# One-hot columns made by ScalarE alone, GpSimd left with gathers, and coefficient lines written at the head of their step

## The reference, cut to what matters

```python
def peer_ffn(h, w_q, sub_keys, u_tab, v_tab):
    q = einsum('bsd,dk->bsk', h, w_q)                  # 8 heads, two halves of 128
    scores = einsum('bshcd,hcnd->bshcn', q, sub_keys)  # 128 keys for each half
    s1, i1 = top_k(scores[..., 0, :], 16)
    s2, i2 = top_k(scores[..., 1, :], 16)
    top_s, pos = top_k(s1[..., :, None] + s2[..., None, :], 16)
    ids = i1 * 128 + i2                                # at pos
    gates = softmax(top_s)
    act = gelu(einsum('td,tkd->tk', hx, u_tab[ids])) * gates
    return einsum('tk,tkd->td', act, v_tab[ids])
```

## Time and profile before

| | us |
|---|---|
| median of 3 runs | 3553.94 |
| lowest and highest | 3546.19, 3554.21 |
| the profiled execution | 3556.24 |
| its span in the trace | 3554.20 |
| first step of `build_experts` to the end of step 17 | 993 to 1562 |
| steps 6 to 14 (groups and quads) | 1120 to 1478 |
| steps 15 to 17 (groups alone) | 1478 to 1562 |

### The profile page before, as it was taken

The page is one execution under the profiler, slowest core; times in us unless marked ns, Lnnn a source line. Parts: engine busy times, 40 slices in busy tenths (PEclk is TensorE's granted clock), DMA queues, the critical chain, the costliest instruction groups (busy, mean ns, idle before and its releaser), DMA issues.

```text
span 3554.2 us, 32041 instructions
## 1 busy us (share of the span) xinstructions
PE 2922.2 (82%) x10195; PEld 1434.4 (40%) x10195; DVE 1954.6 (55%) x4610; ACT 558.1 (16%) x1043; POOL 1588.2 (45%) x1444
## 2 busy tenths in 40 slices
PE   8999999785245766666758999989999899998997
PEld 3455455443122333443323444434444344443333
DVE  2334433787579777867874656645556444443103
ACT  1321133221002444640000000000000000000000
POOL 0010011334434555454456565555666566664441
PEclk9999969877577888777879999999999999999998
DMA  2100121444687888679899999999999999998993
GB/s 102 46 24 24 37 74 51 146 146 144 225 299 252 307 305 318 232 268 372 311 344 405 397 404 401 402 349 391 389 404 374 356 394 401 402 406 343 336 349 117
DMA packets 307573, 981.52 MB, mean 276 GB/s; under 512 B 29904, under 2 KB 57680, under 8 KB 306640
## 3 DMA queue, kind: packets, MB, share of 16 engines
q0 software_dynamic: 184320, 671.17, 50.2%
q1 hardware_dynamic: 120464, 307.85, 22.9%
q10 hardware_dynamic: 2624, 0.46, 0.1%
HBM read 941.63 MB, written 37.75 MB: 276 GB/s over the span
## 4 chain that ended last, share of the span: by engine, by line
PE 25%; DMA 16%; DVE 11%; POOL 11%; issue 7%; ACT 1%; DVEq 1%; ACTq 0%; SPq 0%; another core or an unknown queue 0%; POOLq 0%
DMA v_ring<-in_peer_v_dram,ids_t 11%; PE part L1703 8%; PE hid L1684 7%; PE acc L1736 6%; POOL v_ring L1630 5%; POOL u_ring L1621 4%; DVE u_ring L1976 4%; DMA u_ring<-in_peer_u_dram,ids_u 3%; PE turn_ps L1676 3%; POOL dense_sums L1652 1%; PE part L1712 1%; DMA wq_pair<-in_peer_wq_dram 1%; DVE scratch_later L1215 1%; DVE scratch_later L1213 1%; DVE idx_later L1162 1%
## 5 line engine op out<-in xcount | busy, mean ns | idle before, releaser
L1976 DVE CUSTOM_DVE_ANT_0 u_ring<-u_ring,x_rows_in 128x1024 f32<-128x1024 f32 x560 | 678.1, 1227 | 511.2 <-DMA u_ring<-in_peer_u_dram,ids_u 477.9
L1630 POOL DMA_INDIRECT v_ring<-in_peer_v_dram,ids_t x640 | 678.8, 1061 | 577.1 <-PE acc L1736 415.5
L1621 POOL DMA_INDIRECT u_ring<-in_peer_u_dram,ids_u x560 | 620.4, 1108 | 461.2 <-DVE dots L1976 325.7
L1703 PE MATMUL part<-room 128*128 128x512 f32 x1536 | 694.6, 603 | 83.9 <-DVE room L1956 76.5
L1684 PE MATMUL hid<-x1t_dense,room 128*128 128x384 f32 x2048 | 703.5, 497 | 10.8 <-DMA room<-in_peer_ut_dram 9.0
L1684 PEld LDWEIGHTS hid<-x1t_dense,room 128*128 128x128 f32 x2048 | 386.9, 193 | 349.2 <-issue 107.1
L1736 PE MATMUL acc<-v_ring,line 128*32 128x512 f32 x2560 | 350.2, 669 | 184.7 <-DMA v_ring<-in_peer_v_dram,ids_t 132.2
L1703 PEld LDWEIGHTS part<-room 128*128 128x128 f32 x1536 | 292.8, 193 | 445.7 <-issue 343.1
L1799 ACT ACTIVATE room<-hid 128x384 f32<-128x384 f32 x128 | 62.7, 490 | 1555.3 <-PE hid L1684 1368.4
L1966 DVE TENSOR_TENSOR dense_sums<-dense_sums,part 128x512 f32<-128x512 f32 x186 | 125.6, 685 | 297.3 <-PE part L1703 258.9
L1736 PEld LDWEIGHTS acc<-v_ring,line 128*32 128x32 f32 x2560 | 75.7, 117 | 398.7 <-issue 338.3
(11 more groups left out here) (312 smaller groups left out, 2734.8 us busy)
## 6 DMA issues: line engine op xcount, KB each, us to landing
wq_pair<-in_peer_wq_dram SPq DMA_DIRECT2D x32, 2048.0 KB
room<-in_peer_ut_dram SPq DMA_DIRECT2D x128, 512.0 KB
room<-in_peer_v_dram SPq DMA_DIRECT2D x128, 512.0 KB
gate_grid<-room SPq DMA_DIRECT2D x6, 4096.0 KB, 15.1
room<-gate_grid SPq DMA_DIRECT2D x32, 768.0 KB
w_ring<-in_w_in_dram SPq DMA_DIRECT2D x5, 2048.0 KB, 8.0
v_ring<-in_peer_v_dram,ids_t POOLq DMA_INDIRECT x640
u_ring<-in_peer_u_dram,ids_u POOLq DMA_INDIRECT x560
```

The source lines that it names most:

```text
L1621: pool.indirect_dma_start(u_ring[:, n % U_RING, :], None, peer_u, bass.IndirectOffsetOnAxis(ap=ids_u[:, q, k:k + 1], axis=0))\
L1630: pool.indirect_dma_start(v_ring[:, n % V_RING, :], None, peer_v, bass.IndirectOffsetOnAxis(ap=ids_t[:, q % 2, token:token + 1], axis=0))\
L1703: last = mm.matmul(part[k % 3][:], weights[:, n % 2, i, d * P:(d + 1) * P], vd[:, slot, half * 512:(half + 1) * 512], start=(i == 0), stop ...
L1976: vec.tensor_tensor_reduce(u_ring[:, n % U_RING, :], u_ring[:, n % U_RING, :], x1[:, q % 2, :], 1.0, 0.0, ALU.mult, ALU.add, dots[:, q % 2 ...
```

## The change

- GpSimd's subtraction (L1652) and its semaphore are gone. GpSimd's program in `build_experts` holds gathers and nothing else after its constants.
- `parts_t` now holds i1, the gate and minus i2, in this order. The third is copied out of PSUM with scale -1 by an instruction of its own, so there are two copies for a dense tile where there was one.
- `mark_i2` makes |0..127 - i2| by ScalarE alone: four instructions of 128x128, one for each token, with the token's column of minus i2 as bias, and then the relu over 128x512 as before. It waits for the group three before to have been built instead of for GpSimd.
- A line other than a tile's first is written at the head of the step that holds its first quad, ahead of everything else that ScalarE does in that step. A tile's first line stays where it was, since its coefficients come only in the same quarter.
- ScalarE waits at its start for the seventh constant, the row 0..127.

```diff
-                    for k in share(token_groups(s), i, PARTS):
-                        d, at = k // QUADS, (k % QUADS) * 4
-                        pool.wait_ge(parts_t_ready, d + 1)
-                        if k >= HELD:
-                            pool.wait_ge(group_built, k - HELD + 1)
-                        pool.tensor_tensor(is_i2[:, k % HELD, :, :], iota[:].unsqueeze(1).broadcast_to([P, 4, P]),
-                                           parts_t[:, d % 2, 1, at:at + 4].unsqueeze(2).broadcast_to([P, 4, P]), ALU.subtract)\
-                            .then_inc(from_i2_ready, 1)
...
             def mark_i2(k):
-                act.wait_ge(from_i2_ready, k + 1)
+                d, at = k // QUADS, (k % QUADS) * 4
                 near = is_i2[:, k % HELD, :, :].rearrange("p j n -> p (j n)")
-                act_.activation(near, near, ACT.Abs)
+                if k >= HELD:
+                    act.wait_ge(group_built, k - HELD + 1)
+                for j in range(4):
+                    act_.activation(is_i2[:, k % HELD, j, :], iota[:], ACT.Abs, bias=parts_t[:, d % 2, 2, at + j:at + j + 1])
                 act.drain()
                 act_.activation(near, near, ACT.Relu, bias=1.0, scale=-1.0).then_inc(i2_ready, 1)
 
+            def write_line(q, i):
+                n = q * LINES + i // LINE_QUADS
+                if n >= 2:
+                    act.wait_ge(quads_used, (n - 1) * LINE_QUADS)
+                entries = line[:, n % 2, 0:LINE_QUADS * 4 * 32].rearrange("p (s j k) -> p s j k", s=LINE_QUADS, j=4)
+                act_.activation(entries[:, :, :, 31], coef_t[:].rearrange("p (j s) -> p s j", j=4)[:, i:i + LINE_QUADS, :], ACT.Copy)\
+                    .then_inc(line_ready, 1)
+
             for s in range(STEPS):
                 pick, c, groups = chosen_pair(s), dense_chunk(s), token_groups(s)
+                for m, q, i in quads_at(s):
+                    if i % LINE_QUADS == 0 and i:
+                        write_line(q, i)
...
                     for m, q, i in quads_in(s, quarter):
-                        if i % LINE_QUADS == 0:
-                            n = q * LINES + i // LINE_QUADS
-                            if n >= 2:
-                                act.wait_ge(quads_used, (n - 1) * LINE_QUADS)
...
+                        if i == 0:
+                            write_line(q, i)
...
-                        act_.activation(parts_t[:, d % 2, :, :].rearrange("p c n -> p (c n)"), turn_ps[:, 0:3 * P], ACT.Copy)
+                        act_.activation(parts_t[:, d % 2, 0:2, :].rearrange("p c n -> p (c n)"), turn_ps[:, 0:2 * P], ACT.Copy)
+                        act_.activation(parts_t[:, d % 2, 2, :], turn_ps[:, 2 * P:3 * P], ACT.Copy, scale=-1.0)
```

More of the change, by code:

```diff
@@ L1460, in build_experts @@
         part_added = sem("part_added_e")
-        from_i2_ready = sem("from_i2_ready_e")
         i2_ready = sem("i2_ready_e")
@@ L1756, in _ @@
                         d = DENSE.index(t)
-                        for i, src in enumerate((parts[:, d % 2, 0, :], parts[:, d % 2, 1, :], gates[:, gates_row(t), :])):
+                        for i, src in enumerate((parts[:, d % 2, 0, :], gates[:, gates_row(t), :], parts[:, d % 2, 1, :])):
                             last = mm.transpose(turn_ps[:, i * P:(i + 1) * P], src, ident[:])
@@ L1818, in _ @@
                     for m, q, i in quads_in(s, quarter):
-                        if i % LINE_QUADS == 0:
-                            n = q * LINES + i // LINE_QUADS
-                            if n >= 2:
-                                act.wait_ge(quads_used, (n - 1) * LINE_QUADS)
-                            entries = line[:, n % 2, 0:LINE_QUADS * 4 * 32].rearrange("p (s j k) -> p s j k", s=LINE_QUADS, j=4)
-                            act_.activation(entries[:, :, :, 31], coef_t[:].rearrange("p (j s) -> p s j", j=4)[:, i:i + LINE_QUADS, :], ACT.Copy)\
-                                .then_inc(line_ready, 1)
+                        if i == 0:
+                            write_line(q, i)
                 if (t := tile_chosen(s, 1)) is not None:
@@ L1984, in _ @@
                             last = vec.tensor_scalar(is_i1[:, k % HELD, j, :], iota[:], parts_t[:, d % 2, 0, at + j:at + j + 1],
-                                                     parts_t[:, d % 2, 2, at + j:at + j + 1], ALU.is_equal, ALU.mult)
+                                                     parts_t[:, d % 2, 1, at + j:at + j + 1], ALU.is_equal, ALU.mult)
                         last.then_inc(i1_ready, 1)
```

2 lines of the change are left out of this document (1 added, 1 removed).

## The result

The changed kernel takes 3497.79 us in the median of 4 runs (3491.37 to 3499.85); the kernel before, on the same chip, 3554.07 (3546.19 to 3556.77). The ratio is 0.984, with a 95% interval of 0.9826 to 0.9854. The profiled execution of the changed kernel took 3491.37 us, with a span of 3489.6 and a mean granted clock of 0.904.

A forecast was written before the change was run, and what follows sets the result against it. In steps 6 to 14 ACT waits for POOL, POOL for PE and PE for ACT; from 1800 us on PE and DMA are nearly full. Terms 31 + 7 + 8 - 2 + 3 = 47 us gave 3507 us, range 3482 to 3535.

The forecast's parts named there:

- The likeliest case: Whole kernel: the forecast itself, 3507 us, within 3495 to 3522, given a chance of 0.60.
- The sum of the lap: Steps 6 to 14: moved lines and removed subtractions together save 38 us, with 70 us the most the stretch could give.
- 31 for the lines: Steps 6 to 14: seven moved lines let their quads start 4.4 us sooner each, 31 us, bounds 17 and 43.
- The start of quad 16: Step 10 on PE: quad 16 starts within 2 to 5 us of its last gather's issue plus 3.8.
- the rows are the bound: Sign of being wrong: quads still start 8 us or more behind their last gather.
- The rival that said so: Late-line quads wait for rows instead, laps stay nearly as long: 20 us gained, 3534 us; chance 0.16.
- Subtractions out of POOL: Steps 6 to 14: each quad's rows issued 1.0 us faster, counting in 7 laps: 7 us, bounds 0 and 16.
- VectorE less disturbed in steps 15 to 17: Steps 15 to 17: i1 tiles and key choice no longer stretched by POOL's subtractions, 8 us, bounds 3 and 12.
- one more of my marks of being wrong: Sign of being wrong: ACT's marks are what PE's groups wait for.
- The slower rival: Steps 6 to 17: ACT becomes the bound; a 5 us turn makes them 50 us longer, 3604 us; chance 0.05.
- +3 for its rest: Step 6 between quads 0 and 1: groups no longer wait for POOL, 3 us gained, bounds 0 and 4.
- -2 for the marks ahead of quad 0: Step 6: seven longer ACT marks ahead of the first line delay quad 0, a loss of 2 us, bounds 0 and 5.

The follow-up runs named there:

- e1: The kernel before with only the lines moved to the head of their step, GpSimd still subtracting: 3515.94 us, ratio 0.9881 to the kernel before.
- e2: The changed kernel with its lines back at their old place behind the marks: 3504.66 us, ratio 0.9853 to the kernel before.
- e6: The changed kernel with tile 0's gathers fetching only 2 KB of each 4 KB row, so the output is not the reference's: 3460.30 us, one run.
- e7: The changed kernel plus 96 unused GpSimd subtractions, each waiting for the group three before: 3522.35 us, ratio 0.9918 to the kernel before.
- e10: The changed kernel run again unaltered, to see how well stages repeat: 3494.13 us, ratio 0.9844 to the kernel before.
- e5: The changed kernel with every mark's four absolute values made twice on ScalarE: 3530.72 us, ratio 0.9931 to the kernel before.
- e3: The changed kernel plus 96 unused GpSimd subtractions at their old places, waiting for no other engine: 3525.90 us, ratio 0.9925 to the kernel before.

## Why the prediction was right, and where it was not

The forecast was 3507 (3482 to 3535), faster; measured were 3497.8 and, the second time, 3494.1. The likeliest case held, in its place and about in its size.

- **Where the time lies.** It said steps 6 to 14 in 320 us with a DMA share of 0.89, steps 15 to 17 in 76. Measured: 317.6 and 320.3 with 0.88 and 0.87, and 74.4 and 74.6. The dense steps kept their length within what varies anyway, and the gain reached the end through the chain of the earlier trace rows.
- **The sum of the lap, 38 us.** Steps 7 to 13 lost 39.1. The size was right; its split into 31 for the lines and 7 for the subtractions was wrong as a sum of two terms, and that these two add up to what was measured is in part luck. By e1 the lines alone give 35 us in these steps, by e2 the marks alone 38, both 39. I had seen that ACT waits for POOL, POOL for PE and PE for ACT, and yet priced the removal of the ACT-to-POOL link only by the 1.0 us of issue that it saves, as if a ring had to be cut twice. There is also a slip in the working: 1314.25 - 1307.7 is 6.5 us and not 6.2, which would make the lines 32 us and changes nothing else.
- **What the 39 us are.** TensorE's waits at the seven quads with a late line fell from 46.3 to 31.0 us, those at the other quads from 36.3 to 23.8, and its busy time in these steps from 195.5 to 189.3 us, at a granted clock of 0.87 where it was 0.82. For the last two the prediction had only the 7 us of faster issue; the clock had no term.
- **The start of quad 16.** It was to start 2 to 5 us behind the time that its last issue + 3.8 gives. It was 5.2 (9.0 - 3.8), just outside, and so one of my own marks for "the rows are the bound" came true (8 us or more behind the last gather). By e6 the rows are indeed the bound now. The rival that said so was right in its mechanism, since the seven quads still wait, and now for their rows, and near in its price for them: 2.5 us each, where these waits shrank by 2.2. It was wrong in that the laps would stay nearly as long: it gave nothing for GpSimd, and the other quads wait 12.5 us less.
- **Subtractions out of POOL.** Gathers stand 1.24 us apart, as said (1.26). Their worth of 7 us in steps 6 to 14 was near, taken by itself: e7 against the changed kernel gives 10 us there (7.5 against e10), with both causes in it, the issue (5.9 to 4.8 us a quad) and VectorE's stretch. "In steps 6 to 14 DVE waits anyway and this is hidden" is therefore not shown, and it isn't refuted either: how the 10 us divide between the two stays open.
- **VectorE less disturbed in steps 15 to 17.** 8 us were forecast; by e1 against the changed kernel, and by e7, it is 10, of which the i1 tiles are 7 to 9.
- **ScalarE.** Four absolute values took 1.23 to 1.26 us, where I had taken 1.2 and the nearest row gave 1.14; the turn in step 10 is 2.71 us, under 2.9. By my estimate from the rule of the Trainium skill ("ScalarE: Activation LUTs", *What ACT_TABLE_LOAD costs*) one takes 387 ns and four 1.27 us; the trace agrees, with a mean of 386 ns. That ScalarE hides it was right for steps 7 to 13. For steps 15 to 17 one more of my marks of being wrong came true: TensorE's groups wait there for ScalarE's marks, 17.6 us where it was 5.3. The stage still lost its 10 us, with ScalarE and VectorE level. The slower rival was to decide at a turn of 4.5 us; e5, with 2.7 + 1.2 = 3.9, already lost 33 us in the median, and in its trace, whose execution lies 6.5 us above that median, 39.6 us in steps 6, 14 and 15 to 17. So that point lay too high for these steps: I had taken the mean step of 37 us as ScalarE's room, and steps 15 to 17 last 25.
- **Step 6.** +3 for its rest and -2 for the marks ahead of quad 0 were to give +1. Steps 5 and 6 together went from 58.1 to 59.4: no gain. The term "rest of step 6" is the one that the trace doesn't bear out. The second quad did come closer to the first, 8.6 us where it was 10.2:

```profile
1138.29 2.63 PE L1727 MATMUL acc<-v_ring,line 128*32 128x512 f32 x16 [2.03 <-ACT line L1775]
...
1146.89 1.93 PE L1727 MATMUL acc<-v_ring,line 128*32 128x512 f32 x16
```

but the first waited longer for its line (2.03 us, was 1.10). Both are as small as what varies from trace to trace.

## What to carry to other kernels

When the waits of the engines close a ring, price the cut of the ring once, whichever link is cut, and then look for what is late next; the worth of each link changes with what else is late (the line edit: 38 us alone, nothing that can be told on top of the marks, 15 with the quads spread). After such a cut look at once at how the load is spread over the steps, for that was worth another 34 us here and was a change of one line. Whether an engine can take more work is told by its busy time against the shortest step that it has to fit into, not against the mean step. A helper's work on GpSimd is paid twice, in what stands behind it in its own queue and in what it takes from VectorE.

## What the runs showed of the hardware that was not expected

- **VectorE and GpSimd take turns.** I expected a stretch; I did not expect it to be so regular. In the burst of e3 the second eight i1 tiles of VectorE (1.12 us for four undisturbed) took 1.08 us each, about one subtraction of GpSimd (1.13 us). In the kernel before, 54 of the 384 tiles overlap a subtraction; they take 1.38 us in the mean, the other 330 take 0.35. The Trainium skill ("SBUF — State Buffer", *Who interferes with whom*) says of VectorE in a perf mode that uses two ports, which it says `tensor_scalar` can enter, that it contends with GpSimd: whoever issues first gets the shared pair of ports for the whole instruction and the other is blocked fully. The trace agrees in that one tile passes for each subtraction; that the tiles run in this mode no run here shows.
- **Gathers disturb VectorE little.** In the changed kernel, in which GpSimd issues nothing but gathers, an i1 tile takes 356 ns in the mean over steps 6 to 17, against 491 with the subtractions: 369 ns where it overlaps a gather and 345 where GpSimd is idle. It is the arithmetic on GpSimd that costs, not its being busy.
- **Rows land late when DMA is full.** 128 rows of 4 KB, four times, landed for quad 16 by 9.0 us behind the last issue, with DMA at 9 tenths or more in all but one slice of that time and another transfer beside them, and 3.8 us behind when gathers ran alone in the kernel before.
